# RWKV branch of a hybrid encoder layer: its two halves staged one after the other, or beside each other

## The reference

```python
w = -softplus(-(w0 + tanh(wd) @ w2)) - 0.5
decay = exp(-exp(w)); a = sigmoid(a0 + ad @ a2)
kk = l2norm(k * k_k); k = k * (1.0 + (a - 1.0) * k_a)
a_vec, b_vec = -kk, kk * a
def step(S, inp):                       # one token; S is 64 x 64 per head
    sa = einsum('bhvk,bhk->bhv', S, a_t)
    S = S * w_t + sa (x) b_t + v_t (x) k_t
    return S, einsum('bhvk,bhk->bhv', S, r_t)
y = group_norm(y) * ln_w + ln_b + sum(r * k * r_k) * v
# then: y * silu gate, concatenated with the S5 branch, @ w_out, + x
```

## Time and profile before

| | us |
|---|---|
| median of three runs | 1712.02 (1711.22 to 1713.32) |
| the profiled execution | 1713.09 |
| its span | 1711.3 |
| busy: PE / PEld | 1290.9 / 1079.7 |
| busy: DVE / ACT / POOL | 952.9 / 441.5 / 340.0 |
| RWKV branch, from the trace's 1161.6 to 1605.6 | 444.0 |

### The profile page before, as it was taken

One profiled execution on the slowest core, in us unless ns is written; L12 is line 12 of the kernel. 1 busy time (PEld: TensorE's weight loads), 2 busy tenths in 40 slices (PEclk: granted clock), 3 DMA queues, 4 the chain that ended last, 5 costly groups with the idle time before them and its releaser, 6 DMA issues. The chain is left out here.

```text
span 1711.3 us, 20261 instructions
## 1 busy us (share of the span) xinstructions
PE 1290.9 (75%) x8242; PEld 1079.7 (63%) x8242; DVE 952.9 (56%) x1299; ACT 441.5 (26%) x698; POOL 340.0 (20%) x178
## 2 busy tenths in 40 slices
PE   3999999956671869947997999993418833379498
PEld 2688878825571857736886888881418812279376
DVE  5377510146579346147975656746894478953731
ACT  5222321242331233033332212212212222222400
POOL 2232212104360025012311111210300004000310
PEclk9999999987795788967999999997666966659699
DMA  5222231030000012353331416221000000000322
GB/s 163 40 48 60 68 87 49 25 123 20 1 1 1 1 40 97 98 173 86 101 98 57 124 43 179 62 74 61 1 1 26 1 0 0 1 26 1 123 74 98
DMA packets 117988, 99.85 MB, mean 58 GB/s; under 512 B 37064, under 2 KB 102600, under 8 KB 117768
## 3 DMA queue, kind: packets, MB, share of 16 engines
q1 hardware_dynamic: 104552, 80.60, 16.0%
q10 hardware_dynamic: 13344, 17.96, 3.2%
HBM read 73.38 MB, written 23.46 MB: 57 GB/s over the span
## 5 line engine op out<-in xcount | busy, mean ns | idle before, releaser
L167 PE MATMUL banks<-xt_lo,w_hi 128*128 128x512 f32 x816 | 320.5, 393 | 8.0 <-POOL w_lo L421 8.0
L168 PE MATMUL banks<-xt_hi,w_lo 128*128 128x512 f32 x816 | 318.5, 390 | 0.0
L169 PE MATMUL banks<-xt_hi,w_hi 128*128 128x512 f32 x816 | 318.4, 390 | 0.0
L421 POOL TENSOR_TENSOR w_lo<-features,w_hi 128x1024 fp32r<-128x1024 f32 x55 | 148.3, 2697 | 474.0 <-ACT w_hi L430 474.0
L167 PEld LDWEIGHTS banks<-xt_lo,w_hi 128*128 128x128 f32 x816 | 153.7, 188 | 42.7 <-POOL w_lo L421 9.1
L169 PEld LDWEIGHTS banks<-xt_hi,w_hi 128*128 128x128 f32 x816 | 153.6, 188 | 32.1
L168 PEld LDWEIGHTS banks<-xt_hi,w_lo 128*128 128x128 f32 x816 | 153.8, 188 | 31.5
L470 ACT ACTIVATE temporaries<-banks 128x1024 f32<-128x1024 f32 x45 | 54.0, 1200 | 331.6 <-PE banks L169 315.8
L730 PE MATMUL banks<-features,big 32*32 32x32 f32 (+1 forms) x576 | 32.3, 262 | 118.3 <-DVE features L696 118.3
L730 PEld LDWEIGHTS banks<-features,big 32*32 32x32 f32 (+1 forms) x576 | 31.2, 175 | 119.1 <-DVE features L696 118.8
L1324 DVE TENSOR_TENSOR temporaries<-temporaries,banks 128x1024 f32<-128x1024 f32 x16 | 19.5, 1221 | 127.4 <-PE banks L169 109.7
(11 more groups left out here) (407 smaller groups left out, 2678.6 us busy)
## 6 DMA issues: line engine op xcount, KB each, us to landing
features<-in_even_w_in SPq DMA_DIRECT2D x26, 512.0 KB, 3.9
features<-in_odd_w_in SPq DMA_DIRECT2D x25, 512.0 KB, 4.5
features<-in_x SPq DMA_DIRECT2D x8, 512.0 KB, 4.5
even_gates<-temporaries ACTq DMA_DIRECT2D x8, 512.0 KB, 2.6
features<-even_gates SPq DMA_DIRECT2D x8, 512.0 KB, 7.7
features<-in_even_w_out SPq DMA_DIRECT2D x8, 512.0 KB, 3.3
temporaries<-in_x SPq DMA_DIRECT2D x8, 512.0 KB, 4.1
h_between_layers<-temporaries SPq DMA_DIRECT2D x8, 512.0 KB, 5.0
```

The costliest lines, as they stand in the source:

```text
L167: nc.tensor.matmul(out, w[0], x[1], start=start, stop=False)
L168: nc.tensor.matmul(out, w[1], x[0], start=False, stop=False)
L169: return nc.tensor.matmul(out, w[0], x[0], start=False, stop=stop)
L421: nc.gpsimd.tensor_tensor(wl[n % 2], wr[n % NW], wh[n % 2].bitcast(F32), ALU.subtract).then_inc(low, 1)
```

## The change

1. The RWKV branch becomes five blocks instead of fourteen. `side_by_side` builds one block from several programs. Every program is a set of generators, one for each engine, that yield a due number ahead of each step; `in_turn` issues at each point the step with the lowest due number. So the order within an engine is fixed when the kernel is built, and an engine still waits in order.

```diff
+def in_turn(eng, *programs):
+    steps = [program(eng) for program in programs]
+    due = [next(step, NEVER) for step in steps]
+    while min(due, default=NEVER) < NEVER:
+        i = due.index(min(due))
+        due[i] = next(steps[i], NEVER)
...
-    r7_start(co)
-    for half in range(2):
-        f = R7(co, half)
-        r7_features(co, half)
-        norm_blocks(co, f"rn{half}", ..., beside=r7_decay(co, half), fetch=[(zc[b], oc[b]) ...] if half == 0 else ())
-        r7_apply_decay(co, half)
-        r7_pairs(co, half)
-        invert(co, f"ri{half}", store_slot(co, 1), R7_INVERT)
-        r7_state(co, half, zg)
-        r7_finish(co, half)
+    first, second = R7(co, 0), R7(co, 1)
+    side_by_side(co, clearing(co), r7_prepare(co, first, 0))
+    side_by_side(co, clearing(co), invert(co, "ri0", first.n_st, R7_INVERT[0], narrow=True), r7_prepare(co, second, 33))
+    side_by_side(co, clearing(co), r7_state(co, first), invert(co, "ri1", second.n_st, R7_INVERT[1], narrow=True, pace=lambda t: 1.5 * t))
+    side_by_side(co, clearing(co), gates_of(co, zg), r7_state(co, second), r7_finish(co, first, gated=(co.gates_in, 64)))
+    ahead = [(co.at(A_F[4] + 1024 * i, (D,)), w_out[i * P:(i + 1) * P, :], sem) for i, sem in enumerate(w_in)]
+    side_by_side(co, clearing(co), r7_finish(co, second), out_ahead(co, [(zc[b], oc[b]) for b in range(WB)], ahead))
+    project_out(..., ahead=w_in)
```

```diff
+    def scalar(act):                                       # r7_prepare; d = 0 or 33
+        for j in range(2):
+            yield 1 + 7 * j                                # two tanh, then five scalings or squares
...
+        for j in range(2):
+            yield d + 8 + 6 * j
+            act.wait_ge(centred, j + 1)
+            nc.scalar.activation(x.g[j], x.centred[j], ACT.Exp).then_inc(e0_out, 1)
+            act.wait_ge(shifted, j + 1)
+            nc.scalar.activation(x.centred[j], x.centred[j], ACT.Exp, scale=-1.0).then_inc(e1_out, 1)
+            nc.scalar.activation(x.late[j], x.late[j], ACT.Exp).then_inc(e2_out, 1)
+        yield d + 17                                       # Sqrt of the norms
+        yield d + 21                                       # high parts
+        for c0, c1 in ((0, 3), (3, 6), (6, 8)):            # diagonal blocks, 4 copies each
+    def gpsimd(pool):
+        for j in range(2):
+            pool.wait_ge(centred, j + 1)
+            pool.wait_ge(bonus, j + 1)
+            nc.gpsimd.tensor_tensor(x.late[j], x.centred[j], x.lw[j], ALU.subtract).then_inc(shifted, 1)
+        for j in range(2):
+            pool.wait_ge(normed, j + 1)
+            nc.gpsimd.tensor_tensor(x.b[:, j, :], x.b[:, j, :], x.kk[:, j, :], ALU.mult).then_inc(b_rated, 1)
+        if half == 1:                                      # clears n_st and the two rings
+    def vector(dve):
...
+        for c in range(NT):
+            yield d + 34.5 + c
+            dve.wait_ge(pairs_made, c + 1)
+            nc.vector.copy_predicated(x.n_st[:, 4 * c:4 * c + 4, :] ..., strict ..., banks(c)[:, :, 0:2 * P] ...).then_inc(kept, 1)
```

4. `r7_state` makes the other three score matrices itself, per chunk, one chunk ahead, into a ring of two (cleared once in all). PSUM banks are shared by the two blocks `j`, and R, SA, the state update and the output copy treat both blocks in one instruction:

```diff
+        def pairs(c, j):                                   # PE: 2 heads x 3 matmuls of 64 x 128 x 128
+        def keep(c, j):                                    # DVE: 2 copy_predicated of 128 x 384
...
+            yield 10 * c                                   # PE: wait tok_out, kept, updated; read
+            yield 10 * c + 1                               # PE: turn(c + 1, 0), pairs(c + 1, 0)
+            yield 10 * c + 3                               # PE: wait r_out; solve
+            yield 10 * c + 4                               # PE: out
+            yield 10 * c + 6                               # PE: wait sa_out; grown; ys
+            yield 10 * c + 7                               # PE: turn(c + 1, 1), pairs(c + 1, 1)
...
+            yield 10 * c + 1                               # DVE: wait rs; R copy
+            yield 10 * c + 3                               # DVE: keep(c + 1, 0)
+            yield 10 * c + 7                               # DVE: wait grown; 2 adds, 2 products
+            yield 10 * c + 8                               # DVE: keep(c + 1, 1)
```

6. `project_out`, in both layers, has the second group of tiles in another order:

```diff
-            for g in range(NT // 4):
-                for k in range(KT):
...
-                    for i in range(4):
-                        if g and k == 0:
-                            pe.wait_ge(added, i + 1)
+            for k in range(KT):
+                pe.wait_ge(low_m, k + 1)
+                pe.wait_ge(low_w, k + 1)
+                for t in range(4):
+                    products(t, k)
+            for t in range(4, NT):
+                pe.wait_ge(added, t - 3)
+                for k in range(KT):
+                    products(t, k)
```

More of the change, by code:

```diff
@@ L1949, in r7_decay @@
     startm = co.at(A_CST + C_START, (T,))
     v3 = lambda ap: ap.rearrange("p (c t) -> p c t", t=P)
-    e = x.factors
+    banks = lambda i: co.ps[:, 2 + 2 * (i % 3):4 + 2 * (i % 3), :]
+    wide = lambda i: banks(i).rearrange("p h t -> p (h t)")
+    sq = [co.at(A_T + 1024 * j, (T,)) for j in range(2)]
+    rows = co.at(A_T + 2048, (Q,))
+    high, low = co.row_parts
+    pairs = co.pairs_r
+    scale, eps = (co.at(A_CST + C_PARAM + 4 + i, (1,)) for i in range(2))
+    own_quarter = co.at(A_CST + C_QUARTER, (4,))
@@ new lines, in vector @@
+        yield d + 20
+        dve.wait_ge(rooted, 1)
+        nc.vector.reciprocal(rows, rows).then_inc(inverted, 1)
+        yield d + 21.5
+        dve.wait_ge(inverted, 1)
+        for q, (_, of) in enumerate(quarters):
+            dve.wait_ge(high_r, q + 1)
+            nc.vector.scalar_tensor_tensor(low[:, of], rows, own_quarter[:, q:q + 1], high[:, of].bitcast(F32), ALU.mult, ALU.subtract).then_inc(low_r, 1)
+        for j in range(2):
+            yield d + 23 + 1.5 * j
+            dve.wait_ge(spread, j + 1)
+            v = x.kk[:, j, :].rearrange("p (h t) -> p h t", h=2)
+            tt(v, v, banks(1 + j), ALU.mult).then_inc(normed, 1)
@@ L2063, in r7_state @@
[L2063 to L2071 removed]
+    S, R, SA = (co.at(A_T + 1536 + 256 * i, (2, P)) for i in range(3))
@@ new lines, in r7_state @@
+    zeroed, turned, tok_out, pairs_made, kept, rs, r_out, solved, sa_out, ys, y_out, grown, added, updated = (
+        co.sem(f"r7s{half}_{y}") for y in ("zeroed", "turned", "tok_out", "pairs_made", "kept", "rs", "r_out", "solved", "sa_out", "ys", "y_out", "grown", "added", "updated"))
+    both = lambda b: co.ps[:, b, 0:2 * P].rearrange("p (j t) -> p j t", j=2)
+    turns, read, solve, out = co.ps[:, 2, 0:3 * P], both(3), both(4), both(5)
+    scores = lambda h: co.ps[:, 6 + h % 2, 0:3 * P]
+    halves = [slice(0, 64), slice(64, 128)]
@@ new lines, in scalar, with take @@
+    def scalar(act):
+        def take(c, j):
+            act.wait_ge(turned, 2 * c + j + 1)
+            if c >= 2:
+                act.wait_ge(ys, c - 1)
+            nc.scalar.activation(tok[j][c % 2], turns.rearrange("p (i t) -> p i t", i=3), ACT.Copy).then_inc(tok_out, 1)
+        yield -1
+        take(0, 0)
+        take(0, 1)
+        for c in range(NT):
+            if c + 1 < NT:
+                yield 10 * c + 2
+                take(c + 1, 0)
+            yield 10 * c + 4
+            act.wait_ge(solved, c + 1)
+            if c:
+                act.wait_ge(ys, c)
+            nc.scalar.activation(SA, solve, ACT.Copy, scale=-1.0).then_inc(sa_out, 1)
+            yield 10 * c + 8
+            act.wait_ge(ys, c + 1)
+            nc.scalar.activation(x.kk[:, :, c * P:(c + 1) * P], out, ACT.Copy).then_inc(y_out, 1)
+            if c + 1 < NT:
+                yield 10 * c + 9
+                take(c + 1, 1)
@@ L2172, in r7_state, with out_ahead, sync @@
-    co.release(old)
-def r7_finish(co, half, ahead=()):
+        sp.wait_ge(gates_in, 16 * 4)
+    co.gates_in = gates_in
+    return dict(sync=sync)
+def out_ahead(co, loads, ahead):
+    zc_in = co.sem("zc_in")
+    def sync(sp):
+        yield 0
+        for dst, src, sem in ahead:
+            sp.dma_start(dst, src).then_inc(sem, 16)
+        for dst, src in loads:
+            sp.dma_start(dst, src).then_inc(zc_in, 16)
+        sp.wait_ge(zc_in, 16 * len(loads))
+    return dict(sync=sync)
```

867 lines of the change are left out of this document (468 added, 399 removed).

## The result

The changed kernel takes 1641.93 us (median of 4 runs, 1631.34 to 1657.82) against 1712.28 (4 runs, 1711.22 to 1713.32); the ratio is 0.957, 95% interval 0.953 to 0.961. The forecast was 1590 with 1560 to 1628. The spread is new: the runs of the kernel before lie within 0.6% of each other, these within 1.6%, and the time goes with the granted clock (1631.34 at 0.880, 1636.63 at 0.878, 1647.22 at 0.873, 1657.82 at 0.864). The profiled execution is the fastest of them, with a span of 1629.6, so the trace misses the forecast by 41 us, and the median by 52.

A forecast was written before the change was run, and what follows sets the result against it. DVE was taken to bound all branch stages but the state, which PE bounds, with barriers keeping them apart. Five blocks of 334.5 us replace 444.0 (109.5 less), output matmuls save 12.7: from 1713.09 to 1590, range 1560 to 1628.

The forecast's parts named there:

- C: Block with half 0's state beside half 1's inversion: 92 us (81 to 108) in place of 113.2.
- 36.5 + 5.5 x 3.5: Term of C while the inversion's chain runs: DVE's chain plus 3.5 us for each of 5.5 chunks, 56 us.
- low-clock rival: Pauses in C and D get TensorE only 1.2 GHz: C + 26, D + 46, whole 1662 us; chance 0.07.
- intermediate outcome: Remark in the low-clock rival: the score stage's clock of 0.84, PE busy three quarters of it, speaks for a partial loss.
- C or D at clock 0.5 to 0.7: Sign set beforehand that would show the forecast wrong: that granted clock in either block, against 0.85 or more expected.
- D: Block with half 1's state beside half 0's finish: 72 us (64 to 84) in place of 76.5.
- A: Block with the preparation of half 0: 56 us (50 to 63) in place of 91.6.
- The bonus matmuls end at 19.9: Step in A's path: bonus matmuls end 19.9 us into the block, then two POOL subtractions end at 26.5.
- B: Block with half 0's inversion beside half 1's preparation: DVE sum 82 plus 11 of waits, 93 us, replacing 141.7.
- E: Block with the finish of half 1, weight transfers hidden beside it: 21.5 us (21 to 37).
- the output matmuls: Odd and even output matmuls, by reordering and weights loaded ahead: 7.7 and 5.0 us less, together 12.7 (9 to 14).
- all ends: Sum of all ends of A to E: 299 to 398 us, given as 1551 to 1657 for the whole kernel.

The follow-up runs named there:

- fill_var: Changed kernel plus matmuls that nothing reads, before the reads of half 0's state loop (0, 0, 5, 5, 5, 5, 2, 2 by chunk): 1626.76 us, ratio 0.950.
- serial_all: Changed kernel with every program of B, C and D in a block of its own, nothing of one half beside the other: 1720.25 us, ratio 1.0045 to the kernel before.
- bonus_fill: `fill_var` with the first block's bonus product moved ahead of the second block's sums of squares on TensorE in the preparation: 1638.57 us (1624.40 to 1647.99).
- packed: Changed kernel with C's inversion chain given due numbers only between the early masked copy and the state's update of each chunk, no work added: 1676.22 us.
- pause_d: Changed kernel with three DVE passes ahead of one pair of late masked copies in D, to make one TensorE pause: 1641.27 us.
- pace12: Changed kernel with half 1's inversion interleaved in C at pace 1.2 in place of 1.5: 1653.9 us, one run at 1626.94, five from 1651.65 to 1655.12.
- no_scores: Changed kernel with the three score matrices made for the first chunk only, so the output isn't the reference's: 1627.95 us.
- fill_mid: Changed kernel plus five matmuls that nothing reads before the reads of chunks 2 to 5 in half 0's state loop: 1638.69 us (1633.46 to 1660.04).

## Why the prediction was wrong, step by step

- **C, 22 of the 44 us: the failed step.** The sum took DVE to set the time while the chain runs, "36.5 + 5.5 x 3.5", and the records' durations to stay as in the earlier trace rows of a loop at 0.95. DVE's work was sized rightly (72 busy, 73 forecast). But DVE, where it sets the time, leaves TensorE pauses of over 2 us, and behind each TensorE is granted half its clock for most of the next chunk. By the terms of the sum: the stretch beside the chain took 67.5 us (1323.5 to 1391.0, at 0.74) and not 56, and in `fill_var`, with its pauses filled, 59.3. The start took 9.3 and not 4, at 0.54 behind a pause of 4.2 us at the barrier, and no version changed that. What is left behind the chain took 37.6 at 1.00 and not 32.5, which is a size and no clock. By the busy times and clocks of the chunks, the low clock costs up to 8 us in C's first two chunks and 12 in the next four (an estimate: busy time times one less the clock, by chunk). Filling got back 8 of the 12 by the traces. The low-clock rival stood in the prediction with "intermediate outcome" beside it and a chance of 0.07. Its argument against, "PE has 7.3 us of work in each 9 to 10 us", is a mean and says nothing of a single pause, and the sign set for it, "C or D at clock 0.5 to 0.7", was not met either: a mean of 0.81 in C hides stretches of 12 to 13 us at 0.50. The Trainium skill (TensorE: Matmul & The Clock Gate, "HAM oscillation") tells of a loop whose pauses cost the clock anew in each turn, there through waits for a DMA. C's trace agrees for waits on DVE, in two of its chunks: pauses of 2.25 and 2.54 us, each with 12 to 13 us at 0.50.
- **The runs above the trace, 11 us of the median.** Between the traces of different versions C's tail or D's start keeps the clock or loses it, for 20 us and more. That the longer runs of one version lose it there too is argued, from their lower mean clocks; none of them was traced. A range for one fixed time had no room for it.
- **D, 8.6: a size.** D took 10.1 us a chunk, not 9.0. The twelve score records of half a chunk take 1.26, 0.105 each in place of 0.081, and all scores together 2.4 a chunk in place of 1.95. The late copies, last in the order, hold the next read for 0.92, a wait that the sum lacked; but with them moved forward (`early_keep`) a chunk at the full clock was only 0.2 shorter, so that wait is not the bulk of it. `serial_all` has 9.66 for each chunk at 1.00 with nothing beside it; the finish's transposes add 0.8 to two of them.

```profile
1450.08 1.26 PE L2222 MATMUL banks<-features 64*128 64x128 f32 x12
1452.26 0.46 PE L2240 MATMUL banks<-temporaries,features 128*128 128x128 f32 x2 [0.92 <-issue]
```

- **A, 4.7: a size.** "The bonus matmuls end at 19.9" was the end of ACT's passes (19.5 measured); two DVE products and 3 us of matmuls lie behind it, and they end at 25.3. Moving POOL's work or TensorE's order didn't shorten it.

```profile
1172.80 4.74 PE L2026 MATMUL banks<-big 128*128 128x512 f32 x8
1175.97 5.65 POOL L2101 TENSOR_TENSOR big<-big 128x1024 f32<-128x1024 f32 x2 [13.90 <-PE banks L2026]
```

- **B, 8.3: inside the forecast's own 83 to 106, cause open.** DVE is at 79.15, near the 82 forecast, so waits make 22 us and not 11. They stand at the joins and behind POOL. Work begun earlier made B longer; with POOL's subtractions on DVE (`pool_dve`) it was 1.7 us shorter, and nothing else that was tried shortened it.

```profile
1284.45 0.68 DVE L761 COPY big<-banks 64x512 f32<-64x512 f32 x1 [2.90 <-PE banks L785]
1301.70 1.22 DVE L2168 TENSOR_TENSOR features<-features,big 128x1024 f32<-128x1024 f32 x1 [2.24 <-POOL features L2105]
```

- **Right:** E (21.9 against 21.5), the last adds 10.9 us apart with no DMA wait, nothing from the even inversion, and that the halves overlap. That the output matmuls gave 12.8 where 12.7 were forecast is in part luck: the start of the odd one gave 1.3 us less and the two ends 1.4 more. One sum is off without a consequence: the lower end of all ends, 1551, is 1553 by its own terms.

Why the same pause of about 1 us at the barrier keeps the clock in one program and loses it in another stays open, and so does a layout that needs no wasted matmuls.

## What to carry to other kernels

When a change lays vector work beside a matmul loop, look at the pauses of TensorE in it, one by one, and not only at its mean load: here pauses of 2.3 to 2.5 us cost another 5 to 6 us each, and a clock lost ahead of the inversion's tail stayed lost for 50 us and more. A kernel whose runs spread over 26 us, where those of the kernel before stay within 10, may owe it to such a loop; compare all of its runs then, and not one. Filling the pause with matmuls that nothing reads is a cheap test of it, and gave the best version here as well. It didn't secure the clock everywhere: `bonus_fill`, with the same matmuls in C and D, still ran from 1624 to 1648.

## What the runs showed of the hardware

- With TensorE busy for 63 of 65 us in small matmuls of the inversion's tail and the state, the granted clock stayed at 0.50 (`packed`); in the changed kernel the same tail, entered at 1.00, stayed at 1.00 (37.6 us).
- Pauses of TensorE of 2.25, 2.54 (changed kernel) and 2.34 us (`pause_d`) were followed by 10 to 13 us at 0.50. One of 1.69 us in C of `pace12` (1375.1 to 1376.8) was not, and in `no_scores`, a loop with less work, the clock fell 2.3 us after one of 1.3.
- The same order of matmuls behind a barrier pause of 1.04 us was granted 1.00 in one program and 0.64, then 0.50, in another (on another chip); so it was with the changed kernel and `fill_mid`.
- Beside one POOL subtraction a DVE product took 2.90 us in place of 1.22 (`bonus_fill`), so starting POOL earlier gained nothing.
- Two DVE passes over 1024 columns beside two POOL products took 5.86 us in the odd `project_out`, where one alone took 1.23 in the kernel before.
- ACT passes over 1024 columns with a scale for each partition took 1.13 to 1.24 us against 1.05 without.
